# Triangular inversion of the gated delta rule: four doublings on four 32x32 blocks instead of five on two 64x64 blocks

## The chip, the cores and the metric

The kernel runs on one core of a Trainium2 chip. The metric is the device time of one execution in microseconds. TensorE (PE in the profile) multiplies, VectorE (DVE), ScalarE (ACT) and GpSimd (POOL) do the elementwise work, and SyncE (SP) issues the transfers.

## The reference

One decoder layer over 512 positions of width 1024. The normalised input goes through one projection of about 11,300 columns into three branches (differential attention, gated delta rule, cross-attention into 256 memory positions); three output projections are merged by gates, then comes one more projection, and a squared-ReLU MLP of width 4096. The change lies in the gated delta rule of branch B:

```
C = DN_CHUNK                                   # 64 positions in the reference
decay = jnp.exp(jnp.where(causal, G[..., :, None] - G[..., None, :], -jnp.inf))
lower = jnp.where(strict, jnp.einsum('bhnid,bhnjd->bhnij', k_beta, k) * decay, 0.0)
rhs = jnp.concatenate([v_beta, k_beta * jnp.exp(G)[..., None]], axis=-1)
sol = lax.linalg.triangular_solve(lower + jnp.eye(C, dtype=f32), rhs, left_side=True,
                                  lower=True, unit_diagonal=True)
```

The solution is unique in exact arithmetic whatever the length of a chunk; the kernel works with chunks of 128 positions.

## The kernel before, in words

**The weight stream.** All projections are sequences of tiles: 128 output channels by 512 positions (256 for the memory), 8 blocks of 128 input channels each. Every fp32 product is made of three fp32r products (high times high, high times low, low times high), lines L1688 to L1690, into `acc`. The work is cut into pieces of a quarter of a tile (half a tile for the memory), and between two pieces TensorE takes one step of the attention (`attn`, into `ps_a`) or of the delta rule (`delta`, into `ps_d`).

**The delta rule** runs four times, once per pair of heads p. A pair has 2 heads x 4 chunks = 8 matrices of 128x128, and most steps treat all 8 with one small matmul each. `delta_steps()` lists the steps. dv, dk, dq, dqT, dqd, dkT, dkb and dO are transposes; dE, dL, dA, dU and dW are products of 8 full 128x128 matrices; sa and sb are the recurrence over chunks. dL gives the strictly lower matrix (transposed, in `LT`), and between dA and dU its unit triangular system is inverted.

**The inversion** doubles the size of the inverted diagonal blocks: with T the inverse for blocks of one size, the next is T (I - L_level T), L_level being L under a mask that leaves the squares off the diagonal inside blocks of twice the size. So each level has a step Za (L_level times T, subtracted from the unit matrices as it leaves PSUM, giving Y) and a step Wb (Y times T, and the same transposed). T1 is Za of the first level. Levels 1 to 5 work on the two 64x64 blocks of the diagonal of each of the 8 matrices; Zl and Wl then compute the one 64x64 block off the diagonal. The masked matrices of each level (`XT[0]`, `XT[1]`, in buffers SCR and KBT) are made by one 128x1024 operation per level, the first on VectorE (L1491), five on GpSimd (`level_operand`, L883).

**The array.** A matmul whose operands begin at partition 0 or 64 and have 64 rows and 64 output partitions takes one 64x64 tile of the array, so that two on the diagonal can run together. In T1 and Za the two write to different banks (`block_out`), in Wb too (L1817 bank 0, L1820 bank 1).

**The order.** `plan_order` computes ahead of time, from `ORDER` (the sequence of weight tiles) and the tables `PE_US`, `ACT_US`, `DVE_US`, `POOL_US` (planned times), in which order each engine's queue holds its work. In the program that order is fixed, and semaphores carry the dependencies: a step on TensorE waits for the evacuation of the step before it, except as `vector_before` and `pool_before` say. A step that is not ready holds up the weight stream behind it.

## Time and profile before

| | |
|---|---|
| median of 3 runs | 1416.65 us (1414.28 to 1417.52) |
| profiled execution, its own time | 1417.36 us |
| its span, first to last instruction | 1415.5 us |
| TensorE busy | 1380.3 us, 98% |
| VectorE, ScalarE, GpSimd busy | 805.6, 475.2, 245.2 us |
| chain that ended last, share of PE | 93% |

The projections of the mixing part and, between their pieces, all attention and delta steps lie between the start-up and 841 us; the branch outputs, the merge and the MLP follow. A matmul's record begins when it starts to stream and its duration includes the way through the array, so the records of a row overlap; distances between starts tell what a matmul costs the queue. An fp32 matmul leaves two records.

### The profile page before, as it was taken

The page shows a single profiled execution, that of the slowest core. Times are in us where ns is not written, and L with a number is a line of the kernel's source. Part 1 is how long each engine was busy: PE and PEld are TensorE (multiplying, and loading weights), DVE is VectorE, ACT ScalarE, POOL GpSimd, SP SyncE. Part 2 cuts the span into 40 slices and gives each one's busy share as a digit, 9 for nine tenths or more (in the row PEclk, how much of TensorE's full clock was granted, in tenths as well). Part 3 has the DMA queues.
Part 4 walks back from the last instruction along what each step waited for, and adds up shares of the span by engine and source line. Part 5 has one row for each costly group of instructions (what it writes and reads, how often), then busy time and mean ns, then how long its engine had stood idle before and what let it go on. Part 6 is the DMA issues. An engine that isn't in the chain of part 4 may idle for free.

```text
span 1415.5 us, 20801 instructions
## 1 busy us (share of the span) xinstructions
PE 1380.3 (98%) x8692; PEld 1145.9 (81%) x8692; DVE 805.6 (57%) x1264; ACT 475.2 (34%) x742; POOL 245.2 (17%) x156
## 2 busy tenths in 40 slices
PE   5999999999999999999999999999989999999998
PEld 5689887788888888788887878888878888888886
DVE  6796325588935787767865444454356532355342
ACT  5344333334334434444334321122443221232231
POOL 1113100004200122001330142223222200022010
PEclk9999999999999999999999999999989999999998
DMA  5154212222212321123222356644313223322221
GB/s 208 60 178 143 91 60 75 95 85 82 70 60 75 112 68 61 53 68 104 83 68 69 119 180 207 193 157 143 118 45 105 91 88 97 99 102 89 90 89 60
DMA packets 46420, 142.91 MB, mean 101 GB/s; under 512 B 4944, under 2 KB 7416, under 8 KB 46328
## 3 DMA queue, kind: packets, MB, share of 16 engines
q1 hardware_dynamic: 46328, 141.59, 30.1%
q8 instruction: 69, 1.13, 0.3%
q14 instruction: 23, 0.19, 0.0%
HBM read 126.88 MB, written 16.27 MB: 101 GB/s over the span
## 4 chain that ended last, share of the span: by engine, by line
PE 93%; DVE 5%; ACT 1%; issue 1%; DMA 0%; DVEq 0%; POOL 0%; SPq 0%; ACTq 0%
PE acc L1688 25%; PE acc L1690 24%; PE acc L1689 24%; PE ps_d L1830 2%; PE ps_d L1812 2%; PE ps_d L1817 2%; PE ps_a L1763 2%; PE ps_a L1774 1%; PE ps_d L1802 1%; PE ps_d L1820 1%; DVE conv_y L1383 1%; PE ps_a L1742 1%; PE ps_a L1753 1%; DVE w_lo L1285 1%; PE ps_d L1797 1%; PE ps_a L1769 1%
## 5 line engine op out<-in xcount | busy, mean ns | idle before, releaser
L1688 PE MATMUL acc<-n_hi,w_hi 128*128 128x512 f32 (+1 forms) x984 | 396.7, 403 | 7.4 <-DVE n_lo L1310 4.3
L1690 PE MATMUL acc<-n_hi,w_lo 128*128 128x512 f32 (+1 forms) x984 | 383.3, 390 | 0.0
L1689 PE MATMUL acc<-n_lo,w_hi 128*128 128x512 f32 (+1 forms) x984 | 382.9, 389 | 0.0
L1285 DVE TENSOR_TENSOR w_lo<-w_raw,w_hi 128x1024 fp32r<-128x1024 f32 x200 | 284.4, 1429 | 141.9 <-ACT w_hi L996 141.3
L996 ACT CAST w_hi<-w_raw 128x1024 fp32r<-128x1024 f32 x200 | 209.4, 1048 | 456.3 <-PE acc L1690 456.3
L1688 PEld LDWEIGHTS acc<-n_hi,w_hi 128*128 128x128 f32 x984 | 188.0, 191 | 49.0 <-issue 8.8
L1690 PEld LDWEIGHTS acc<-n_hi,w_lo 128*128 128x128 f32 x984 | 187.7, 191 | 40.5
L1689 PEld LDWEIGHTS acc<-n_lo,w_hi 128*128 128x128 f32 x984 | 188.4, 191 | 34.7 <-issue 0.2
L1690 PE MATMUL acc<-h_hi,w_lo 128*128 128x512 f32 x256 | 101.0, 395 | 0.0
L1688 PE MATMUL acc<-h_hi,w_hi 128*128 128x512 f32 x256 | 101.0, 395 | 0.0
L1689 PE MATMUL acc<-h_lo,w_hi 128*128 128x512 f32 x256 | 101.0, 395 | 0.0
L984 POOL TENSOR_TENSOR h_lo<-sq,h_hi 128x512 fp32r<-128x512 f32 x32 | 41.4, 1293 | 234.0 <-DVE h_hi L1619 234.0
L1688 PE MATMUL acc<-y_hi,w_hi 128*128 128x512 f32 x192 | 76.1, 396 | 0.7 <-ACT gate_st L1075 0.7
L1690 PE MATMUL acc<-y_hi,w_lo 128*128 128x512 f32 x192 | 76.0, 396 | 0.0
L1689 PE MATMUL acc<-y_lo,w_hi 128*128 128x512 f32 x192 | 76.0, 396 | 0.0
L926 POOL TENSOR_SCALAR gate_st<-gate_st 128x512 f32<-128x512 f32 x24 | 25.1, 1045 | 286.8 <-ACT gate_st L1075 286.8
L1230 ACT ACTIVATE sq<-relu 128x512 f32<-128x512 f32 x32 | 20.2, 632 | 125.2 <-DVE relu L1617 125.2
L1383 DVE SCALAR_TENSOR_TENSOR conv_y<-conv_x,par,conv_y 128x512 f32<-128x512 f32 x72 | 59.4, 825 | 2.6
L1690 PEld LDWEIGHTS acc<-h_hi,w_lo 128*128 128x128 f32 x256 | 48.2, 188 | 11.3
L1688 PEld LDWEIGHTS acc<-h_hi,w_hi 128*128 128x128 f32 x256 | 48.2, 188 | 11.2
L1689 PEld LDWEIGHTS acc<-h_lo,w_hi 128*128 128x128 f32 x256 | 48.2, 188 | 11.2
L1617 DVE TENSOR_SCALAR relu<-acc 128x512 f32<-128x512 f32 x31 | 21.4, 691 | 39.8 <-PE acc L1690 39.8
(322 smaller groups left out, 2051.8 us busy)
## 6 DMA issues: line engine op xcount, KB each, us to landing
w_raw<-weights SPq DMA_DIRECT2D x200, 512.0 KB, 3.3
gate_scratch<-gate_st SPq DMA_DIRECT2D x24, 256.0 KB, 2.2
g_in<-gate_scratch SPq DMA_DIRECT2D x24, 256.0 KB, 3.7
y_raw<-y_scratch SPq DMA_DIRECT2D x16, 256.0 KB, 3.5
x_tok<-x SPq DMA_DIRECT2D x4, 512.0 KB, 5.1
y_scratch<-y_st SPq DMA_DIRECT2D x4, 512.0 KB, 3.0
y_scratch<-d_ET SPq DMA_DIRECT2D x4, 512.0 KB, 3.2
y_scratch<-y_st SPq DMA_DIRECT2D x8, 256.0 KB, 3.5
```

What stands on the lines that cost most here:

```text
L926: nc.gpsimd.tensor_scalar(gate_st[:], gate_st[:], 0.5, 0.5, ALU.mult, ALU.add).then_inc(gs_ready, 1)
L984: nc.gpsimd.tensor_tensor(h_lo[:, f % 16], sq[:, f % 2], h_hi[:, f % 16].bitcast(F32), ALU.subtract).then_inc(hl_ok, 1)
L996: nc.scalar.copy(w_hi[:, t % SPL], w_raw[:, t % RAW]).then_inc(hi_ready, 1)
L1285: V_.tensor_tensor(w_lo[:, t % SPL], w_raw[:, t % RAW], w_hi[:, t % SPL].bitcast(F32), ALU.subtract).then_inc(lo_ready, 1)
L1383: ins = V_.scalar_tensor_tensor(out=y, in0=conv_x[:, n % 2, j:j + S], scalar=par[:, col + j:col + j + 1], in1=y, op0=ALU.mult, op1=ALU.add)
L1688: mm(bank, wh, hi_of(k), start=start and k == 0, stop=False)
L1689: mm(bank, wh, lo_of(k), start=False, stop=False)
L1690: last = mm(bank, wl, hi_of(k), start=False, stop=stop and k == KT - 1)
L1763: last = mm(ps[:, col:col + (q + 1) * P], qkv_T[rows_m, h % 2, 0, q * P:(q + 1) * P], qkv_T[rows_m, h % 2, 1, 0:(q + 1) * P], start=True, ...
L1812: last = mm(block_out(m, s), XT[c % 2][HP[s], m, HP[s]], right, start=True, stop=True)
L1817: last = mm(ps_d[HP[s], 0, c0:c0 + P // 2], Y[HP[s], m], TP[HP[s], m], start=True, stop=True)
L1830: last = mm(dst[m], a[:, m], b[:, m], start=True, stop=True)
```

## The change

- The levels 1 to 4 (T1, four Za, four Wb) work on the four 32x32 diagonal blocks of each matrix, one matmul per block: 32 per step and product instead of 16. Their operands are packed: 32 columns per matrix, 256 in all, in each buffer. All four blocks of a product go to one bank (`small_out`).
- Level 5 is now two steps like the last level: Z5 and W5 compute the 32x32 blocks off the diagonal inside each 64x64 block. ScalarE puts the result together in TF (six small operations).
- Zl takes its right-hand side from two buffers (TR for the first 32 columns with 64 rows of contraction, TN for the other 32 columns with 32 rows), so it has 16 matmuls instead of 8. Wl is as before.
- ScalarE copies the diagonal blocks of LT into LD (four copies), and one GpSimd operation multiplies LD with the masks of all four levels; five operations fall away. GpSimd clears the whole TF instead of half.
- T1 stands right behind dL in the list of steps. `scalar_before` is new and lets steps wait for an earlier ScalarE part.
- A one-time set-up on VectorE moves mask blocks together and adds up four unit blocks instead of two.
- `ORDER` and the planned times are new, so all queues of the mixing part are ordered anew.

```diff
-         "dkb": "AP", "dL": "DP", "dA": "DP", "T1": "DP", "Za": "DP", "Wb": "AD", "Zl": "A", "Wl": "D",
+         "dkb": "AP", "dL": "ADP", "dA": "DP", "T1": "D", "Za": "D", "Wb": "AD", "Z5": "A", "W5": "AD", "Zl": "A", "Wl": "D",
-PE_US = {"dE": 1.79, "dL": 1.79, "dA": 1.79, "dU": 1.79, "dW": 1.79, "T1": 0.95, "Za": 0.95, "Wb": 1.85, "Zl": 0.95, "Wl": 0.95, "sa": 0.45,
+PE_US = {"dE": 1.79, "dL": 1.79, "dA": 1.79, "dU": 1.79, "dW": 1.79, "T1": 0.55, "Za": 0.55, "Wb": 1.05, "Z5": 0.55, "W5": 0.8, "Zl": 0.95, "Wl": 0.95, "sa": 0.45,
-ACT_US = {"Wb": 0.75, "Zl": 0.62, "sb": 0.45, "cs": 2.9, "as0": 2.3, "as1": 2.9, "at": 1.5, "ap": 0.65,
+ACT_US = {"dL": 1.6, "Wb": 0.45, "Z5": 0.45, "W5": 2.1, "Zl": 0.62, "sb": 0.45, "cs": 2.9, "as0": 2.3, "as1": 2.9, "at": 1.5, "ap": 0.65,
-DVE_US = {"dv": 1.3, "dk": 7.8, "dq": 6.5, "dqT": 1.3, "dL": 2.6, "dA": 2.7, "T1": 0.8, "Za": 0.8, "Wb": 0.8, "Wl": 0.8, "sa": 0.5, "sb": 0.8,
+DVE_US = {"dv": 1.3, "dk": 7.8, "dq": 6.5, "dqT": 1.3, "dL": 2.9, "dA": 1.9, "T1": 0.5, "Za": 0.5, "Wb": 0.6, "W5": 0.5, "Wl": 0.8, "sa": 0.5, "sb": 0.8,
-POOL_US = {"dk": 2.0, "dkT": 2.0, "dkb": 2.0, "dL": 2.5, "dA": 3.8, "T1": 2.5, "Za": 2.5}
+POOL_US = {"dk": 2.0, "dkT": 2.0, "dkb": 2.0, "dL": 2.5, "dA": 4.5}
...
-ORDER = [("conv", 0), ("z", 0), ("gate", 1), ("mem", 0), ("cq", 0), ("cq", 1), ("cq", 2), ("cq", 3),
+ORDER = [("conv", 0), ("gate", 1), ("z", 0), ("mem", 0), ("cq", 0), ("cq", 1), ("cq", 2), ("conv", 1),
...
-        out += [(k, p, 0) for k in ("dv", "dk", "dq", "dE", "dkT", "dkb", "dL", "dqT", "dA", "dqd", "T1")]
-        for lv in range(1, NM - 1):
+        out += [(k, p, 0) for k in ("dv", "dk", "dq", "dE", "dkT", "dkb", "dL", "T1", "dqT", "dA", "dqd")]
+        for lv in range(1, 5):
             out += [("Za", p, lv), ("Wb", p, lv)]
-        out += [("Zl", p, NM - 1), ("Wl", p, NM - 1), ("dU", p, 0), ("dW", p, 0)]
+        out += [("Z5", p, 5), ("W5", p, 5), ("Zl", p, 6), ("Wl", p, 6), ("dU", p, 0), ("dW", p, 0)]
...
-            "dA": ("dL", p, 0), "dqd": ("dqT", p, 0), "T1": ("dqT", p, 0)}.get(kind)
+            "T1": ("dL", p, 0), "dqT": ("dL", p, 0), "dA": ("dL", p, 0), "dqd": ("dqT", p, 0)}.get(kind)
+
+
+def scalar_before(step):
+
+    kind, p, c = step
+    if kind == "Za":
+        return ("dkb", p, 0) if c == 1 else ("dqd", p, 0) if c == 2 else ("Wb", p, c - 2)
+    return {"T1": ("dkb", p, 0), "Z5": ("Wb", p, 3), "Zl": ("Z5", p, 5)}.get(kind)
 
 
 def pool_before(step):
 
     kind, p, c = step
-    if kind == "Za" and c > 2:
-        return ("Za", p, c - 2)
     return {("dE", 0): ("dk", p, 0), ("dW", 0): ("dkb", p, 0), ("sb", 0): ("dA", p, 0),
-            ("Za", 1): ("dL", p, 0), ("Za", 2): ("T1", p, 0), ("dU", 0): ("dA", p, 0)}.get((kind, c))
+            ("Za", 1): ("dL", p, 0), ("dU", 0): ("dA", p, 0)}.get((kind, c))
...
-        XT = (SCR, KBT)
-        TP, TN = (flat(TT[:])[:, n * 512:(n + 1) * 512].rearrange("p (a b) -> p a b", b=P // 2) for n in range(2))
-        Y = flat(KTT[:])[:, 0:512].rearrange("p (a b) -> p a b", b=P // 2)
         HP = (slice(0, P // 2), slice(P // 2, P))
-        two_eyes = cst[:, C_MASK0 + NM - 1, HP[0]]
+        QB = P // 4
+        BLK = [slice(q * QB, (q + 1) * QB) for q in range(4)]
+
+        def part_of(buf, n, width=QB):
+            return flat(buf[:])[:, n * 256:n * 256 + 8 * width].rearrange("p (a b) -> p a b", b=width)
+
+        X0, LD = part_of(KBT, 0), part_of(KBT, 1)
+        XS = flat(SCR[:]).rearrange("p (l a b) -> p l a b", l=4, b=QB)
+        TP, TN, TR = (part_of(TT, n) for n in range(3))
+        Y, Y5, Y6 = part_of(KTT, 0), part_of(KTT, 1), part_of(KTT, 2, P // 2)
+        eyes = cst[:, C_MASK0 + NM - 1, 0:QB]
...
+        def small_out(bank, rows=slice(0, P)):
+
+            return ps_d[rows, bank, 0:256].rearrange("p (a b) -> p a b", b=QB)
+
+        def mid_out(bank, rows):
+
+            return ps_d[rows, bank].rearrange("p (a b) -> p a b", b=P // 2)
...
-                    pool.wait_ge(d_dve, dD[i + 1])
-                    last = level_operand(1)
+                    pool.wait_ge(d_act, dA[i + 1])
+                    last = nc.gpsimd.tensor_tensor(XS, view(LD, [[0, 4], [QB, 8], [1, QB]]),
+                                                   view(cst[:, C_MASK0 + 1, 0:QB], [[P, 4], [0, 8], [1, QB]]), ALU.mult)
                 elif kind == "dA":
                     pool.wait_ge(at_ready, p + 1)
                     nc.gpsimd.tensor_tensor(AT[:], AT[:], over(cst[:, C_UPTO, :], 8), ALU.mult)
-                    last = nc.gpsimd.memset(TF[:, :, HP[0]], 0.0)
-                elif kind == "T1":
-                    pool.wait_ge(d_dve, dD[d_idx[("dA", p, 0)] + 1])
-                    last = level_operand(2)
-                elif kind == "Za":
-                    last = level_operand(lv + 2)
...
+                elif kind == "dL":
+                    act.wait_ge(d_dve, dD[i + 1])
+                    for q in range(4):
+                        last = nc.scalar.copy(LD[BLK[q]], LT[BLK[q], :, BLK[q]])
                 elif kind == "Wb":
-                    for s in range(2):
-                        last = nc.scalar.copy(TF[HP[s], :, HP[s]], whole_bank(0, HP[s]))
+                    last = nc.scalar.copy(TP, small_out(0))
+                elif kind == "Z5":
+                    last = nc.scalar.copy(Y5, small_out(2))
+                elif kind == "W5":
+                    act.wait_ge(d_pool, dP[d_idx[("dA", p, 0)] + 1])
+                    for q in range(4):
+                        nc.scalar.copy(TF[BLK[q], :, BLK[q]], TP[BLK[q]])
+                    for q in (0, 2):
+                        last = nc.scalar.mul(TF[BLK[q], :, BLK[q + 1]], small_out(0, BLK[q]), -1.0)
                 elif kind == "Zl":
-                    last = nc.scalar.copy(by_bank(Y[HP[1]]), blocks_of(HP[1]))
+                    last = nc.scalar.copy(Y6[HP[1]], mid_out(2, HP[1]))
...
-                link(V_.tensor_tensor(two_eyes, ident[:, HP[0]], ident[:, HP[1]], ALU.add))
+                for q in range(1, 4):
+                    V_.tensor_copy(cst[BLK[q], C_MASK0:C_MASK0 + 5, 0:QB], cst[BLK[q], C_MASK0:C_MASK0 + 5, BLK[q]])
+                link(V_.tensor_tensor(eyes, ident[:, BLK[0]], ident[:, BLK[1]], ALU.add))
+                for q in range(2, 4):
+                    link(V_.tensor_tensor(eyes, eyes, ident[:, BLK[q]], ALU.add))
...
-                    last = V_.tensor_tensor(XT[0][:], LT[:], over(cst[:, C_MASK0, :], 8), ALU.mult)
+                    for q in range(4):
+                        last = V_.tensor_tensor(X0[BLK[q]], LT[BLK[q], :, BLK[q]], over(cst[BLK[q], C_MASK0, 0:QB], 8), ALU.mult)
                 elif kind == "dA":
                     V_.tensor_tensor(AT[:], ps, ET[:], ALU.mult).then_inc(at_ready, 1)
-                    for s in range(2):
-                        last = V_.tensor_tensor(TP[HP[s]], over(two_eyes[HP[s]], 8), XT[0][HP[s], :, HP[s]], ALU.subtract)
+                    last = V_.tensor_tensor(TP, over(eyes, 8), X0, ALU.subtract)
                 elif kind in ("T1", "Za"):
-                    eyes = view(two_eyes, [[0, 2], [0, 4], [1, P // 2]])
-                    last = V_.tensor_tensor(by_bank(TN if kind == "T1" else Y), eyes, blocks_of(), ALU.subtract)
+                    last = V_.tensor_tensor(TN if kind == "T1" else Y, over(eyes, 8), small_out(2), ALU.subtract)
                 elif kind == "Wb":
-                    rows = slice(0, P) if c < NM - 2 else HP[0]
-                    last = V_.tensor_copy(TN[rows], whole_bank(1, rows))
+                    last = V_.tensor_copy(TN, small_out(1))
+                    if c == 4:
+                        last = V_.tensor_copy(TR[BLK[0]], small_out(1, BLK[0]))
+                elif kind == "W5":
+                    last = V_.tensor_scalar(TR[BLK[1]], small_out(1, BLK[1]), -1.0, None, ALU.mult)
                 elif kind == "Wl":
-                    last = V_.tensor_scalar(by_bank(TF[HP[0], :, HP[1]]), blocks_of(HP[0]), -1.0, None, ALU.mult)
+                    last = V_.tensor_scalar(TF[HP[0], :, HP[1]], mid_out(0, HP[0]), -1.0, None, ALU.mult)
...
-                    for k in range(8):
-                        for s, m in ((0, k), (1, (k + 4) % 8)):
-                            right = ident[HP[s], HP[s]] if kind == "T1" else TN[HP[s], m]
-                            last = mm(block_out(m, s), XT[c % 2][HP[s], m, HP[s]], right, start=True, stop=True)
+                    for m in range(8):
+                        for b in BLK:
+                            left, right = (X0[b, m], eyes[b]) if kind == "T1" else (XS[b, c - 1, m], TN[b, m])
+                            last = mm(small_out(2, b)[:, m], left, right, start=True, stop=True)
                 elif kind == "Wb":
-                    for s in range(2):
-                        for m in range(8):
-                            c0 = m * (P // 2)
-                            last = mm(ps_d[HP[s], 0, c0:c0 + P // 2], Y[HP[s], m], TP[HP[s], m], start=True, stop=True)
-                            if c < NM - 2 or s == 1:
-                                o = HP[1 - s]
-                                last = mm(ps_d[o, 1, c0:c0 + P // 2], TP[o, m], Y[o, m], start=True, stop=True)
+                    for m in range(8):
+                        for b in BLK:
+                            mm(small_out(0, b)[:, m], Y[b, m], TP[b, m], start=True, stop=True)
+                        for b in BLK:
+                            last = mm(small_out(1, b)[:, m], TP[b, m], Y[b, m], start=True, stop=True)
+                elif kind == "Z5":
+                    for m in range(8):
+                        for q in (0, 2):
+                            last = mm(small_out(2, BLK[q + 1])[:, m], LT[BLK[q], m, BLK[q + 1]], TN[BLK[q], m],
+                                      start=True, stop=True)
+                elif kind == "W5":
+                    for m in range(8):
+                        for q in (0, 2):
+                            mm(small_out(0, BLK[q])[:, m], Y5[BLK[q + 1], m], TP[BLK[q + 1], m], start=True, stop=True)
+                        last = mm(small_out(1, BLK[1])[:, m], TP[BLK[1], m], Y5[BLK[1], m], start=True, stop=True)
                 elif kind == "Zl":
                     for m in range(8):
-                        last = mm(block_out(m, 1), LT[HP[0], m, HP[1]], TN[HP[0], m], start=True, stop=True)
+                        mm(mid_out(2, HP[1])[:, m, 0:QB], LT[HP[0], m, HP[1]], TR[HP[0], m], start=True, stop=True)
+                        last = mm(mid_out(2, HP[1])[:, m, QB:], LT[BLK[1], m, HP[1]], TN[BLK[1], m], start=True, stop=True)
                 elif kind == "Wl":
                     for m in range(8):
-                        last = mm(block_out(m, 0), Y[HP[1], m], TF[HP[1], m, HP[1]], start=True, stop=True)
+                        last = mm(mid_out(0, HP[0])[:, m], Y6[HP[1], m], TF[HP[1], m, HP[1]], start=True, stop=True)
```

Two places on TensorE and one on VectorE, as the programs hold them; names as in the code, `d_` for the buffers of the delta rule, and the last column is what a row writes (xN: N such in a row).

TensorE, the step Wb of level 1 of the first pair, before:

```order
L1688 MATMUL acc<-m_hi,w_hi 128x256
L1689 MATMUL acc<-m_lo,w_hi 128x256
L1690 MATMUL acc<-m_hi,w_lo 128x256
L1817 MATMUL ps_d<-d_TT,d_KTT 64x64
L1820 MATMUL ps_d<-d_KTT,d_TT 64x64
```

and after:

```order
L1698 MATMUL acc<-m_hi,w_hi 128x256
L1699 MATMUL acc<-m_lo,w_hi 128x256
L1700 MATMUL acc<-m_hi,w_lo 128x256
L1828 MATMUL ps_d<-d_TT,d_KTT 32x32 x4
L1830 MATMUL ps_d<-d_KTT,d_TT 32x32 x4
```

The last two rows come 16 times in the one and 8 times in the other program, so the step has 32 matmuls before and 64 after; alternating blocks of 64x64 in two banks have become groups of four blocks in one bank.

TensorE, the step Zl, of the first pair, before:

```order
L1689 MATMUL acc<-n_lo,w_hi 128x512
L1690 MATMUL acc<-n_hi,w_lo 128x512
L1823 MATMUL ps_d<-d_TT,d_LT 64x64 x8
L1688 MATMUL acc<-n_hi,w_hi 128x512
L1689 MATMUL acc<-n_lo,w_hi 128x512
```

and after:

```order
L1699 MATMUL acc<-m_lo,w_hi 128x256
L1700 MATMUL acc<-m_hi,w_lo 128x256
L1843 MATMUL ps_d<-d_TT,d_LT 64x32
L1844 MATMUL ps_d<-d_TT,d_LT 64x32
L1843 MATMUL ps_d<-d_TT,d_LT 64x32
```

L1843 contracts over 64 rows and L1844 over 32; they alternate eight times, where one kind stood in a row.

VectorE, the one-time set-up, before:

```order
L1352 TENSOR_TENSOR smd<-smd 128x1
L1353 TENSOR_SCALAR smd<-smd 128x1
L1355 TENSOR_TENSOR cst<-cst 128x64
L1357 TENSOR_SCALAR beta<-ba 128x32
L1358 TENSOR_SCALAR hbeta<-ba 128x32
```

and after:

```order
L1356 TENSOR_TENSOR smd<-smd 128x1
L1357 TENSOR_SCALAR smd<-smd 128x1
L1360 COPY cst<-cst 32x5x32 x3
L1361 TENSOR_TENSOR cst<-cst 128x32
L1363 TENSOR_TENSOR cst<-cst 128x32 x2
L1365 TENSOR_SCALAR beta<-ba 128x32
```

One addition has become three copies and three additions ahead of the decay's computation.

## Rows read from the trace of the kernel before

**Rows 1.** The page: busy time and share, then TensorE's granted clock in 40 slices.

```profile
PE 1380.3 (98%) x8692; PEld 1145.9 (81%) x8692; DVE 805.6 (57%) x1264; ACT 475.2 (34%) x742; POOL 245.2 (17%) x156
PEclk9999999999999999999999999999989999999998
```

**Rows 2.** Table by window, the mixing part from 60 to 840 us.

```profile
core 0: us, PE busy (x) PEld busy (x) DVE busy (x) ACT busy (x) POOL busy (x), PEclk, DMA share, GB/s
60.00:840.00 780.00, 777.40 (x5882) 648.77 (x5881) 518.00 (x876) 300.58 (x522) 126.11 (x70) 1.00 0.27 90
```

**Rows 3.** Waits of TensorE: waiting line, releaser, us in total, times, longest.

```profile
PE ps_a L1649 <- DVE x_tok L1297: 10.0, 1, 10.0
...
PE ps_d L1797 <- DVE conv_o L1397: 1.2, 1, 1.2
...
PE ps_d L1797 <- DVE d_V L1485: 0.7, 1, 0.7
```

**Rows 4.** Timeline of TensorE, a Wb step: start, us, line, shapes, count.

```profile
136.19 0.28 PE L1690 MATMUL acc<-m_hi,w_lo 128*128 128x256 f32 x1
...
136.51 0.22 PE L1817 MATMUL ps_d<-d_TT,d_KTT 64*64 64x64 f32 x1
136.52 0.22 PE L1820 MATMUL ps_d<-d_KTT,d_TT 64*64 64x64 f32 x1
136.57 0.22 PE L1817 MATMUL ps_d<-d_TT,d_KTT 64*64 64x64 f32 x1
...
138.42 0.38 PE L1688 MATMUL acc<-m_hi,w_hi 128*128 128x256 f32 x1
138.64 0.28 PE L1689 MATMUL acc<-m_lo,w_hi 128*128 128x256 f32 x1
```

**Rows 5.** Timeline of TensorE, the T1 step.

```profile
127.92 0.28 PE L1690 MATMUL acc<-m_hi,w_lo 128*128 128x256 f32 x1
128.13 1.15 PE L1812 MATMUL ps_d<-cst,d_SCR 64*64 64x64 f32 x32
...
129.43 0.28 PE L1689 MATMUL acc<-m_lo,w_hi 128*128 128x256 f32 x1
```

**Rows 6.** Timeline of TensorE, the dL step of full 128x128 matrices.

```profile
109.82 0.28 PE L1690 MATMUL acc<-m_hi,w_lo 128*128 128x256 f32 x1
109.94 1.95 PE L1830 MATMUL ps_d<-d_KBT,d_KTT 128*128 128x128 f32 x16
...
111.84 0.28 PE L1689 MATMUL acc<-m_lo,w_hi 128*128 128x256 f32 x1
```

**Rows 7.** Timeline of TensorE, a score step: 64 rows, 128 columns of the array.

```profile
474.59 0.39 PE L1689 MATMUL acc<-n_lo,w_hi 128*128 128x512 f32 x1
474.82 0.40 PE L1690 MATMUL acc<-n_hi,w_lo 128*128 128x512 f32 x1
475.15 1.56 PE L1763 MATMUL ps_a<-qkv_T 64*128 64x384 f32 x10
...
476.98 0.39 PE L1689 MATMUL acc<-n_lo,w_hi 128*128 128x512 f32 x1
```

**Rows 8.** Timeline of TensorE, the Zl step, one 64x64 tile.

```profile
176.31 0.40 PE L1690 MATMUL acc<-n_hi,w_lo 128*128 128x512 f32 x1
176.64 1.14 PE L1823 MATMUL ps_d<-d_TT,d_LT 64*64 64x64 f32 x16
...
178.05 0.39 PE L1689 MATMUL acc<-n_lo,w_hi 128*128 128x512 f32 x1
```

**Rows 9.** Groups by line and form: busy us, mean ns, idle before, releaser.

```profile
L1506 DVE TENSOR_TENSOR vnew<-d_Q,ps_d 128x256 f32<-128x256 f32 x12 | 5.0, 419 | 14.5 <-PE ps_d L1833 14.5
L1137 ACT COPY d_LT<-ps_d 128x256 f32<-128x256 f32 x16 | 6.0, 373 | 25.7 <-PE ps_d L1843 25.7
L883 POOL TENSOR_TENSOR d_KBT<-d_LT,cst 128x1024 f32<-128x1024 f32 x12 | 28.8, 2400 | 75.7 <-PE ps_d L1812 53.5 <-DVE d_SCR L1491 22.2
```

**Rows 10.** Timeline of VectorE, the one-time set-up.

```profile
61.09 0.22 DVE L1355 TENSOR_TENSOR cst<-cst 128x64 f32<-128x64 f32 x1
```

**Rows 11.** Timeline of GpSimd, its last piece of the first branch's reload.

```profile
837.09 2.21 POOL L920 TENSOR_TENSOR y_lo<-y_st,y_hi 128x512 fp32r<-128x512 f32 x1 [1.53 <-DVE y_hi L1532]
```

More of the change, by code:

```diff
@@ L83 @@
 HOP, MARGIN = 0.2, 0.5
-ORDER = [("conv", 0), ("z", 0), ("gate", 1), ("mem", 0), ("cq", 0), ("cq", 1), ("cq", 2), ("cq", 3),
-         ("conv", 1), ("head", 0), ("gate", 3), ("conv", 2), ("head", 1), ("gate", 2), ("head", 2), ("z", 1),
-         ("gate", 2), ("head", 3), ("head", 4), ("conv", 3), ("head", 5), ("z", 2), ("gate", 2), ("head", 6),
-         ("gate", 3), ("head", 7), ("gate", 2), ("z", 3), ("gate", 9)]
+ORDER = [("conv", 0), ("gate", 1), ("z", 0), ("mem", 0), ("cq", 0), ("cq", 1), ("cq", 2), ("conv", 1),
+         ("gate", 1), ("cq", 3), ("gate", 1), ("head", 0), ("gate", 1), ("conv", 2), ("head", 1), ("gate", 1),
+         ("head", 2), ("z", 1), ("gate", 2), ("head", 3), ("gate", 1), ("head", 4), ("conv", 3), ("head", 5),
+         ("z", 2), ("gate", 3), ("head", 6), ("head", 7), ("gate", 2), ("z", 3), ("gate", 11)]
 def attn_steps():
@@ L257, in plan_order @@
         kind, p, c = s
-        deps = [("ACT", "delta", j) for j in range(i) if "A" in PARTS[delta[j][0]]][-1:]
+        after = scalar_before(s)
+        j = i if after is None else d_idx[after] + 1
+        deps = [("ACT", "delta", j) for j in range(j) if "A" in PARTS[delta[j][0]]][-1:]
         after = vector_before(s)
@@ L279, in plan_order @@
             add("DVE", "delta", ("delta", i), DVE_US["sb_last" if end else kind], deps)
-        if "P" in PARTS[kind] and not (kind == "Za" and c + 2 >= NM - 1):
+        if "P" in PARTS[kind]:
             deps = [mm]
-            if kind == "T1":
-                deps.append(("DVE", "delta", d_idx[("dA", p, 0)]))
             if kind == "dL":
-                deps.append(("DVE", "delta", i))
+                deps.append(("ACT", "delta", i))
             if kind == "dA":
@@ L379, in counts @@
     for s in steps:
-        last_levels = part == "P" and s[0] == "Za" and s[2] + 2 >= NM - 1
-        out.append(out[-1] + (part in PARTS[s[0]] and not last_levels))
+        out.append(out[-1] + (part in PARTS[s[0]]))
     return out
@@ L879, in _ @@
                 nc.gpsimd.tensor_tensor(lo, full[:, j % 4], hi.bitcast(F32), ALU.subtract).then_inc(su_lo, 1)
-            def level_operand(lv):
-                return nc.gpsimd.tensor_tensor(XT[lv % 2][:], LT[:], over(cst[:, C_MASK0 + lv, :], 8), ALU.mult)
             def delta(i):
@@ L887, in delta @@
                 if "P" not in PARTS[kind]:
-                    return
-                if kind == "Za" and lv + 2 >= NM - 1:
                     return
@@ L908, in delta @@
                     nc.gpsimd.tensor_tensor(AT[:], AT[:], over(cst[:, C_UPTO, :], 8), ALU.mult)
-                    last = nc.gpsimd.memset(TF[:, :, HP[0]], 0.0)
-                elif kind == "T1":
-                    pool.wait_ge(d_dve, dD[d_idx[("dA", p, 0)] + 1])
-                    last = level_operand(2)
-                elif kind == "Za":
-                    last = level_operand(lv + 2)
+                    last = nc.gpsimd.memset(TF[:], 0.0)
                 last.then_inc(d_pool, 1)
@@ L1782, in delta @@
                 kind, p, c = DELTA[i]
-                if dA[i]:
-                    pe.wait_ge(d_act, dA[i])
+                before = scalar_before(DELTA[i])
+                n_act = dA[i] if before is None else dA[d_idx[before] + 1]
+                if n_act:
+                    pe.wait_ge(d_act, n_act)
                 before = vector_before(DELTA[i])
```

13 lines of the change are left out of this document (1 added, 12 removed).

## The prediction

> **What bounds the kernel now.** I read the busy shares first: TensorE is busy 1380.3 of 1415.5 us, and the row of its granted clock is 9 nearly throughout, the full 2.4 GHz level, with two slices of 8 [rows 1]. Then the stretch in which all of the change lies, from 60 to 840 us (tables by window): TensorE busy 777.40 of 780.00 us at clock 1.00, VectorE 518.00, ScalarE 300.58, GpSimd 126.11 [rows 2]. Then what TensorE waits for: the long waits are in the start-up, and inside the stretch only 1.2 and 0.7 us stand out, both on VectorE near 78 and 94 us [rows 3]. So TensorE's queue is the path. A microsecond less in it is a microsecond less in the kernel, a microsecond less on the three other engines is worth nothing, and they matter only if they come late.
>
> **What a small step costs today.** I take a step's price as what it inserts between two products of the weight stream: the start of the second product behind it, less the start of the last one ahead, less two normal distances (0.12 us for 256 columns, 0.23 for 512). The last product's successor on either side shows the distances [rows 6, 7].
> - 128x128, 8 matrices, 16 records (each fp32 matmul leaves two): 111.84 - 109.82 - 0.24 = 1.78 us, 0.111 a record, nothing left over [rows 6].
> - T1 or Za, 16 matmuls on two 64x64 tiles: 129.43 - 127.92 - 0.24 = 1.27 us for 32 records, which is 16 turns of two [rows 5].
> - Wb, 32 matmuls: 138.64 - 136.19 - 0.24 = 2.21 us for 32 turns of two [rows 4].
> - Zl, 8 matmuls on one tile: 178.05 - 176.31 - 0.46 = 1.28 us for 16 turns of one [rows 8]. The same as T1: the second tile rides along free.
> The last two sizes give slope and offset: (2.21 - 1.27)/16 = 0.0588 us a turn, and 1.27 - 16 x 0.0588 = 0.33 us a step, which the 128x128 step does not have. I read the 0.33 as two changes of the array's division, 0.165 each. A change of the rows alone costs it too: the score step with 64 rows and all 128 columns inserts 476.98 - 474.82 - 0.46 = 1.70 us [rows 7]; of its ten records four have 128 data columns (0.111 each), two 256 (0.12) and four 384 (0.16 at 2.4 GHz), 1.32 us, and 0.38 are left over.
> Per pair of heads: T1 and five Za 7.62, five Wb 11.05 (I price the last, shorter one alike), Zl and Wl 2.55: 21.2 us.
>
> **What it costs after.** From 128 to 64 a turn fell from 0.111 to 0.0588, by 0.052 for 64 columns of weights and 64 of data. Half of that less gives 0.0326 us for 32x32: an estimate from rows 4 to 6. The number of turns is the program's: 8 matrices x 2 records, whatever the number of blocks, if four blocks share a turn as two do now.
> - T1 and four Za: 5 x (0.33 + 16 x 0.0326) = 4.26 us.
> - Four Wb, 32 turns: 4 x (0.33 + 32 x 0.0326) = 5.49.
> - Z5, 16 turns of two: 0.85. W5: two of its three matmuls for a matrix read the same 32 rows, so 32 turns: 1.37.
> - Zl: it now alternates, per matrix, a matmul with 64 contraction rows and one with 32, so 16 matmuls on one group of columns. Weights are 64 columns and data 32, midway between the two turns: 0.0457 x 32 = 1.46, plus 0.33. And the division changes 15 times inside the step. No row has such a change inside a step. Lower bound: nothing, if only the size 128 against smaller counts; upper: 15 x 0.165 = 2.48 us. I take the upper, since a change of the rows alone is enough in [rows 7]. Zl: 4.27.
> - Wl as now: 1.27.
> Sum 17.5 us a pair, 3.7 less, 14.8 us over four pairs.
>
> **The other engines.** Evacuations shrink from 512 to 256 columns: a 256-column VectorE operation with a PSUM source takes 419 ns, ScalarE's 373 [rows 9]. Five masks of 2400 ns per pair on GpSimd become one; all that was hidden and gains nothing. New: four small copies on ScalarE behind the LT product, about 4 x 0.37 = 1.5 us, then the one GpSimd mask, 2.4. Za 1 waits for it; T1, dqT, dA and dqd with their weight products lie between, at least 0.85 + 0.87 + 1.79 + 0.87 us of steps plus four pieces of the stream at about 1.4 us: some 10 us against 5.1 (1.2 + 1.5 + 2.4). Hidden. W5's ScalarE part is six operations, 2.2 us; Zl doesn't wait for it, only Wl, behind Zl and a piece of the stream: hidden. What is queued behind it on ScalarE is the next weight split, which has whole tiles of slack. If these covers were gone, each would cost its excess, 1 to 2 us a pair.
> The set-up on VectorE (the one-time block at 61 us) has one addition of 0.22 us now [rows 10] and gets three copies and three additions: by bounds 0.22 (64 columns) and 0.42 (256) the copies are about 0.3, the additions 0.2, so +1.3 us. VectorE has no slack there: TensorE's waits of 0.7 and 1.2 us follow [rows 3]. Between nothing and 1.3 I take 1.3.
> The new ORDER moves weight tiles among each other; products and loads stay the same in number. After the last attention step six gate tiles are left instead of seven, 5.5 us less cover for the reload of the first branch. GpSimd now finishes its last y_lo at 839.3 us [rows 11], and that piece is needed 4.8 us after the branch's start near 841.5: margin 7 us, then 1.5. Priced at nothing; gone, it costs up to 2.
> Sum: 14.8 - 1.3 = 13.5 us. The profiled execution took 1417.36 us, 0.71 over the median of the runs shown, so 1403.9 in its terms and **1403 us** in terms of the median.
>
> **A rule against it.** The two records of a pair start at 136.51 and 136.52, about 0.01 us apart, and the turn is 0.0588, so two starts average 0.029 us [rows 4]. Now the two blocks of a turn write to different PSUM banks; after it, four write to one bank, in different partitions. The Trainium skill, TensorEngine Tiling (Array Packing), Restrictions and Gotchas, says that different row tiles cannot access the same bank at once. TensorE: Matmul & The Clock Gate, Part 1, gives about 25 ns as the least distance of starts. By an estimate with that page's 25 ns per start the four-block steps and Z5 and W5 would take the kernel to about 1461 us instead of 1403. The trace shows a shorter distance than this between two tiles, though not on average, and nothing about one bank; what a limit on starts does here is priced from rows as the second rival.
>
> **Rivals.**
> 1. *Changes inside Zl are free.* For: rows 4 to 8 show only changes from and to 128. Against: rows alone suffice [rows 7]. Saves 2.48 x 4 = 9.9 us more: 1393 us.
> 2. *Four blocks don't share a turn: slower.* The mechanism: a start each 0.029 us, the average of today, is the engine's or the bank's limit. Then a turn of four is 0.118: T1 and Za 5 x 2.22 = 11.1, Wb 4 x 4.11 = 16.4, Z5 1.26, W5 1.72, Zl 4.27, Wl 1.27, together 36.0 us a pair, 14.8 more: +59 us, plus the set-up, 1477 us. It decides from a turn of about 0.033 + 3.7/208 = 0.050 us, 208 being the four-block turns of a pair. For: twice as many instructions per step as now, at a rate that no row shows sustained. Against: the 0.01 us inside a pair.
> 3. *The other engines come late or the turn is 0.04 to 0.05.* 13 dependent steps in a shorter chain, now planned against smaller numbers; 0.2 us at each of 52 steps is 10 us: 1413 us. Against: 2.6 us without TensorE work in 780 today [rows 2].
>
> **Numbers.** Chances: forecast 0.40 (its own range 1398 to 1408), rival 1 0.22, rival 2 0.18, rival 3 0.20. The runs shown span 1414.28 to 1417.52, so 0.2% is about what tells from no change: faster means below 1413.8. Faster: 0.40 + 0.22 + 0.12 of rival 3 = 0.74; same 0.05; slower 0.18 + 0.03 = 0.21. The range 1389 to 1418 leaves out rival 2 and the edges of 1 and 3.
>
> **What would show it.** Za's records in turns of four, 0.03 us apart, and the step inserting 0.85 instead of 1.27 us; Zl about 4 us long (rival 1: under 2); no group of small matmuls with a turn above 0.05; TensorE's waits between 60 and 840 us not above 5 us in sum; the end of the gates near 828 us. The forecast is wrong if four blocks queue behind each other, or if the reordered tiles leave TensorE waiting.

## The result, and the profile after

The changed kernel takes 1429.31 us (median of 5 runs, 1423.33 to 1432.13) against 1416.12 of the kernel before (5 runs beside it, 1414.04 to 1417.52): ratio 1.0083, 95% interval 1.0069 to 1.0097. It is slower, where 1403 had been forecast. Its profiled execution took 1424.05 us, 5.3 less than the median of its runs, so the traces below show the loss at its small end.

The page of the kernel after, busy times, TensorE's granted clock, and the queue that carries instructions (packets, MB, share of the DMA engines):

```profile
PE 1370.4 (96%) x10420; PEld 1133.2 (80%) x10420; DVE 772.8 (54%) x1277; ACT 482.7 (34%) x778; POOL 202.2 (14%) x140
PEclk9999999999999999999998999999989999999999
q8 instruction: 83, 1.36, 0.4%
```

The same queue on the page of the kernel before:

```profile
q8 instruction: 69, 1.13, 0.3%
```

TensorE is busy for 9.9 us less than in [rows 1] and the kernel is longer. The table by window says where:

```profile
60.00:840.00 780.00, 761.67 (x7566) 632.47 (x7565) 476.79 (x880) 304.95 (x554) 76.59 (x48) 0.98 0.28 87
530.00:545.00 15.00, 12.70 (x358) 9.64 (x357) 5.43 (x11) 3.55 (x6) 0.00 (x0) 0.89 0.27 86
740.00:785.00 45.00, 43.15 (x592) 34.17 (x591) 16.25 (x35) 14.41 (x28) 1.16 (x1) 0.85 0.21 66
```

Against [rows 2], TensorE now stands idle for 18.3 us of 780 instead of 2.6, and the clock, 1.00 before, is 0.98, with 0.89 and 0.85 in two places. Rows of what it waits for (line, releaser, us, times, longest):

```profile
PE ps_d L1830 <- issue: 4.2, 3, 2.3
PE ps_d L1828 <- issue: 4.2, 4, 1.9
...
PE ps_d L1824 <- issue: 3.0, 4, 1.1
PE acc L1698 <- issue: 2.8, 2, 2.5
...
PE acc L1699 <- issue: 0.9, 1, 0.9
```

These 15.1 us are new beside [rows 3], and their releaser is "issue": no semaphore, no engine. L1824 is T1 and Za, L1828 and L1830 are Wb, L1698 and L1699 are the weight stream. The timeline of TensorE through one Wb (start, us, line, shapes, count):

```profile
144.76 0.28 PE L1700 MATMUL acc<-m_hi,w_lo 128*128 128x256 f32 x1
144.97 0.26 PE L1828 MATMUL ps_d<-d_TT,d_KTT 32*32 32x32 f32 x8
...
145.81 0.21 PE L1828 MATMUL ps_d<-d_TT,d_KTT 32*32 32x32 f32 x2
147.94 0.22 PE L1828 MATMUL ps_d<-d_TT,d_KTT 32*32 32x32 f32 x2 [1.92 <-issue]
...
148.31 0.38 PE L1698 MATMUL acc<-m_hi,w_hi 128*128 128x256 f32 x1
```

and through the next Za:

```profile
149.71 0.28 PE L1700 MATMUL acc<-m_hi,w_lo 128*128 128x256 f32 x1
149.91 0.75 PE L1824 MATMUL ps_d<-d_TT,d_SCR 32*32 32x32 f32 x64
150.60 0.39 PE L1698 MATMUL acc<-m_hi,w_hi 128*128 128x256 f32 x1
150.82 0.28 PE L1699 MATMUL acc<-m_lo,w_hi 128*128 128x256 f32 x1
```

The Za inserts 150.82 - 149.71 - 0.24 = 0.87 us, as forecast (0.85): four blocks do share a turn. The Wb ran at the same pace and then stood still for 2.1 us in the middle of a matrix. The trace has eleven such distances of over 0.7 us between two starts from 100 to 850 us, 16.5 us in all; before has one, 1.05 us.

The trace's records of the instruction queue point to the cause. Each packet has 16,384 bytes; 83 of them for 2 x 10420 TensorE instructions (a load of weights and a matmul each) makes 251 to a packet, the few waits and register instructions not counted. I take it as 256 of 64 bytes; the array probe below, which pauses every 256 instructions, bears this out. Beside the standstills of the first pair:

```
packet starts   takes   TensorE's next start after a standstill
132.98          1.03    135.45
137.23          0.96    139.40
140.56          1.12    143.11
145.18          1.28    147.94
```

Each of the eleven standstills ends 1.1 to 1.6 us after a packet does, and no two packets start less than 3.3 us apart; in the kernel before none start less than 5.3 us apart. A Wb is 256 instructions, issued in 1.1 us.

Zl, beside [rows 8]:

```profile
160.47 0.28 PE L1700 MATMUL acc<-m_hi,w_lo 128*128 128x256 f32 x1
160.67 0.30 PE L1843 MATMUL ps_d<-d_TT,d_LT 64*64 64x32 f32 x2
160.90 0.30 PE L1844 MATMUL ps_d<-d_TT,d_LT 32*64 32x32 f32 x2
...
164.37 0.58 PE L1698 MATMUL acc<-m_hi,w_hi 128*128 128x256 f32 x1
164.75 0.41 PE L1699 MATMUL acc<-m_lo,w_hi 128*128 128x256 f32 x1
164.96 0.41 PE L1700 MATMUL acc<-m_hi,w_lo 128*128 128x256 f32 x1
```

It inserts 4.0 us (4.27 forecast), and behind it the stream's products stand 0.21 us apart instead of 0.12: from 164.2 to 167.6 us the granted clock is 0.5, the 1.2 GHz level. There are five such stretches between 27 and 1030 us where before has none: behind or in Zl of three pairs (3.4, 3.4 and 10.2 us) and behind the two standstills of 2.5 and 1.8 us at 533.6 and 748.6 us (3.4 us each), 23.8 us together. The first product of the branch comes at 850.05 us instead of 841.57, 8.5 later. From there the two kernels take the same time to within 0.4 us up to the last 35 us, in which this execution of the changed kernel is 1.4 us quicker.

### The profile page after: what moved, and what is told of

Same layout as the page of the kernel before. It is cut to its first block, busy times and chain, and to the rows that moved or that the text cites. A ratio compares the mean times of both kernels' runs of the same rounds, so it can differ in the third digit from the quotient of the medians.

```text
span 1422.3 us, 24294 instructions
## 1 busy us (share of the span) xinstructions
PE 1370.4 (96%) x10420; PEld 1133.2 (80%) x10420; DVE 772.8 (54%) x1277; ACT 482.7 (34%) x778; POOL 202.2 (14%) x140
## 4 chain that ended last, share of the span: by engine, by line
PE 91%; DVE 5%; issue 2%; ACT 1%; DMA 0%; DVEq 0%; POOL 0%; SPq 0%; ACTq 0%
PE acc L1698 25%; PE acc L1700 24%; PE acc L1699 24%; PE ps_d L1851 2%; PE ps_a L1773 2%; PE ps_a L1784 1%; PE ps_d L1814 1%; DVE conv_y L1391 1%; PE ps_d L1824 1%; PE ps_a L1763 1%; PE ps_a L1752 1%; DVE w_lo L1289 1%; PE ps_d L1828 1%; PE ps_d L1830 1%; PE ps_d L1809 1%
## 5 line engine op out<-in xcount | busy, mean ns | idle before, releaser
L1698 PE MATMUL acc<-n_hi,w_hi 128*128 128x512 f32 (+1 forms) x984 | 398.2, 405 | 10.8 <-DVE n_lo L1314 4.3
L1699 PE MATMUL acc<-n_lo,w_hi 128*128 128x512 f32 (+1 forms) x984 | 385.0, 391 | 0.0
L1698 PEld LDWEIGHTS acc<-n_hi,w_hi 128*128 128x128 f32 x984 | 188.9, 192 | 48.8 <-issue 8.8
L1699 PEld LDWEIGHTS acc<-n_lo,w_hi 128*128 128x128 f32 x984 | 189.3, 192 | 38.8 <-issue 3.3
L1698 PE MATMUL acc<-h_hi,w_hi 128*128 128x512 f32 x256 | 101.0, 395 | 0.0
L1699 PE MATMUL acc<-h_lo,w_hi 128*128 128x512 f32 x256 | 101.0, 395 | 0.0
L1698 PE MATMUL acc<-y_hi,w_hi 128*128 128x512 f32 x192 | 76.0, 396 | 0.0
L1699 PE MATMUL acc<-y_lo,w_hi 128*128 128x512 f32 x192 | 76.0, 396 | 0.0
L1699 PEld LDWEIGHTS acc<-h_lo,w_hi 128*128 128x128 f32 x256 | 48.2, 188 | 11.3
L1698 PEld LDWEIGHTS acc<-h_hi,w_hi 128*128 128x128 f32 x256 | 48.2, 188 | 11.2
L1698 PEld LDWEIGHTS acc<-y_hi,w_hi 128*128 128x128 f32 x192 | 36.2, 188 | 8.9 <-POOL y_lo L915 0.2
```

What stands on the lines that cost most here:

```text
L1698: mm(bank, wh, hi_of(k), start=start and k == 0, stop=False)
L1699: mm(bank, wh, lo_of(k), start=False, stop=False)
```

## The experiments

Theory F: TensorE passes the array steps faster than its instructions arrive. Theory Z: the alternation in Zl costs more than its own time, through the clock. Rival O: the new order of the stream. Two more rivals stand in the expectations: B, that four blocks which write to one bank hold each other up, and C, that other transfers hold back the packets of instructions.

**Zl in products of one size (zl_one_size).** TR takes 64 columns, a block of it is zeroed, and the second matmul of each matrix goes:

```diff
-mm(mid_out(2, HP[1])[:, m, 0:QB], LT[HP[0], m, HP[1]], TR[HP[0], m], start=True, stop=True)
-last = mm(mid_out(2, HP[1])[:, m, QB:], LT[BLK[1], m, HP[1]], TN[BLK[1], m], start=True, stop=True)
+last = mm(mid_out(2, HP[1])[:, m], LT[HP[0], m, HP[1]], TR[HP[0], m], start=True, stop=True)
...
```

> Zl's right-hand side is put into one buffer of 64 columns per matrix (32 rows of it cleared by GpSimd), so Zl is 8 matmuls of one size again; everything else as in the changed kernel. In the changed kernel's trace Zl inserts 3.95 and 4.08 us where it inserted 1.28 before. Theory Z (the alternation of 64 and 32 contraction rows is paid at every change): Zl inserts 1.3 us, four times 2.7 us less, 10.9 us, and the half-clock window that begins at the first Zl (164 us) goes, 1.7 us: 1416 to 1418 us from 1429. Theory F (TensorE runs out of instructions) alone: the stalls inside Za and Wb stay where they are, 12 to 17 us in sum. Rival O (the cost lies in the new order of the queues): no change, 1429 us.

Measured 1406.55 us (1401.75 to 1412.91), ratio 0.9936 [0.9917, 0.9955]. The timeline of Zl:

```profile
163.29 0.28 PE L1703 MATMUL acc<-m_hi,w_lo 128*128 128x256 f32 x1
163.50 1.14 PE L1846 MATMUL ps_d<-d_TT,d_LT 64*64 64x64 f32 x16
164.57 0.39 PE L1701 MATMUL acc<-m_hi,w_hi 128*128 128x256 f32 x1
164.79 0.28 PE L1702 MATMUL acc<-m_lo,w_hi 128*128 128x256 f32 x1
```

164.79 - 163.29 - 0.24 = 1.26 us, 2.8 less than in this pair above, some 11 over four. Mixing, from the stream's first product to the branch's first, shrank by 21.5 us (829.4 to 807.9), twice that, and the median lies 10 us under the expectation. Ten distances of over 0.7 us remain, 13.4 us in all against 16.5, which is another 3. The rest, some 7.5 us, goes with the clock: one stretch of 3.4 us at half clock is left of 23.8 us. But two of the five stretches had stood behind a standstill and not behind Zl. So Z holds, and more than Zl's own time was saved; how much of the 21.5 us each part gave is an estimate.

**Wb as two steps (wb_in_two).** The order of the stream stays; each Wb is issued as 128 and 128 instructions with a piece of the stream between.

```diff
-out += [("Za", p, lv), ("Wb", p, lv)]
+out += [("Za", p, lv), ("Wa", p, lv), ("Wb", p, lv)]
...
+if e == "PE" and fam == "delta" and delta[q[0][2]][0] == "Wb":
+    ready = max(ready, done[("PE", "delta", q[0][2] - 1)] + 0.6)
```

> The changed kernel with Wb as two steps, its two products of 32 matmuls each, between which the planner is made to put a piece of the weight stream; no matmul more or less. Theory F (a burst of 256 instructions outruns the loads of instructions): costs 16 more entries to the small division at 0.33 us, 5.3 us, and takes the stalls inside Wb away, of 14 to 17 us at least 10, and with them the two half-clock windows at 536 and 751 us, 3.4 us: 1429 + 5 - 10 - 4 = 1420 us, idle of TensorE between 100 and 840 us without a semaphore under 5 us. Rival B (the stalls come from four blocks that write to one bank): the products are the same, so the stalls stay and the entries come on top: 1434 us. Rival O: about 1434 us too.

Measured 1413.37 us (1408.97 to 1418.69), ratio 0.9982 [0.9971, 0.9993], below the expectation. Distances over 0.7 us fell from eleven (16.5 us) to three (3.8 us), and the two half-clock stretches behind the standstills at 533.6 and 748.6 us are gone; 17 us at half clock remain elsewhere. Same instructions, two more changes of the array's division for each Wb, and faster by 15.9 us: F holds, and rival B, which expected 1434, falls.

**The old kernel in the new order (before_new_order).** Only the list ORDER is exchanged; its first rows:

```diff
-ORDER = [("conv", 0), ("z", 0), ("gate", 1), ("mem", 0), ("cq", 0), ("cq", 1), ("cq", 2), ("cq", 3),
+ORDER = [("conv", 0), ("gate", 1), ("z", 0), ("mem", 0), ("cq", 0), ("cq", 1), ("cq", 2), ("conv", 1),
```

> The kernel before with the changed kernel's list ORDER of weight tiles, and its own steps and planned times. Rival O (the new order of tiles makes the other engines late): 1424 to 1430 us. Theories F and Z: the order costs nothing, 1416 us, within 2 us.

Measured 1421.65 us (1420.02 to 1428.19), ratio 1.005 [1.0031, 1.0068]. TensorE's waits:

```profile
PE acc L1688 <- POOL y_lo L920: 4.5, 3, 2.2
```

They stand at 849.7, 851.7 and 854.9 us: the reload of the first branch comes too late, the margin that I had priced at nothing. This profiled execution took 1428.19 us, 6.5 above the median, and has a stretch of 6.8 us at half clock behind these waits, so how much of them the other executions have isn't known. The changed kernel's profile has no wait of this kind. With the shorter steps, mixing and reload meet otherwise.

**The changed kernel in the old order (after_old_order)**: the same exchange, the other way.

```diff
-ORDER = [("conv", 0), ("gate", 1), ("z", 0), ("mem", 0), ("cq", 0), ("cq", 1), ("cq", 2), ("conv", 1),
+ORDER = [("conv", 0), ("z", 0), ("gate", 1), ("mem", 0), ("cq", 0), ("cq", 1), ("cq", 2), ("cq", 3),
```

> The changed kernel with the stream's order list of the kernel before (the list alone; the planner places the steps in it). Theory O (the new list is what costs: before_new_order was 5 us slower than before): 5 us or more below the changed kernel, 1418 to 1424 us. Theory F (the list is innocent, since the changed kernel's profile has none of the waits at L1688 for y_lo, 4.5 us, that before_new_order shows): within 3 us of the changed kernel's 1429 us, as far as the stalls fall alike.

Measured 1424.03 us (1420.05 to 1425.76), ratio 1.0059 [1.0038, 1.008]. Rows of its waits:

```profile
PE ps_d L1828 <- issue: 4.9, 2, 3.2
PE acc L1698 <- POOL y_lo L915: 4.0, 3, 2.3
...
PE ps_d L1824 <- issue: 1.9, 2, 1.1
```

With the old list the changed kernel has 4.0 us of waits for y_lo and fewer "issue" waits. The four medians read as a square: the new steps cost 7.7 us in the old order (1424.03 against 1416.31) and 7.7 in the new (1429.31 against 1421.65); the new list costs 5.6 us with the old steps and 5.3 with the new. So the order is not the main cause, but it is some 5 of the 13 us by which the median rose, more than the 3 that I had allowed. The 5.3 us is not clear of noise: the runs of the changed kernel in its two orders overlap (1420.05 to 1425.76 and 1423.33 to 1432.13). Which wait carries it was not separated.

**The array alone (array_probe).** No layer is computed: TensorE repeats bursts between wide products, without semaphores or other engines, and x is copied to the output. The first burst:

```python
for m in range(64):
    for q in range(4):
        mm(ps[Q4[q], 0, 0:32], a[Q4[q], 0:32], a[Q4[q], 32:64], start=True, stop=True)
```

> A kernel of TensorE bursts alone, without the layer: its output is a copy of x. Between stretches of fp32 128x512 matmuls: 256 matmuls of 32x32 on the four diagonal blocks into one bank; the same into four banks; 256 of 64x64 on two blocks into two banks; 128 of these into one bank; a burst of 32 of 32x32; 16 that alternate 64 and 32 contraction rows; 16 of 64 rows. Theory F: every long burst is bound by the loads of instructions, 1024 instructions in at least four times 2.5 us once the stock is used up, with gaps every 256 instructions of 1 us and more for 32x32 (whose own pace is 1.06 us per 256), none for 64x64 (3.7 us per 256), and the one-bank burst like the four-bank burst. Rival B: the one-bank burst slower per turn than the four-bank one, steadily. Theory Z: 16 alternating matmuls take about 3.7 us, 16 of one size under 1.5. The clock goes to its lower level where the bursts have gaps.

By window: 256 products of 32x32 in four blocks, into one bank; the same into four banks; 256 products of 64x64 in two blocks.

```profile
31.00:43.00 12.00, 6.50 (x514) 5.80 (x512) 0.00 (x0) 0.78 0.02 5
66.00:78.00 12.00, 5.82 (x500) 5.21 (x500) 0.00 (x0) 0.74 0.02 4
101.00:116.00 15.00, 15.00 (x513) 14.98 (x512) 0.00 (x0) 1.00 0.02 4
```

512 records of 32x32 take 11.5 us from first to last start and TensorE works for half of it; the same number of 64x64 takes 14.9 us without a pause. Within the burst a turn of four blocks takes 0.034 us, in one bank as in four, which rules out rival B. But after the first 163 records in the one burst, 243 in the other, and then every 128 (256 instructions), comes a pause of 1.8 to 2.6 us, so such a block takes 3.4 to 3.7 us. A turn of two 64x64 blocks takes 0.0585, so 128 records take 3.7 us, and the supply just keeps up. The clock falls to 0.5 in or behind both bursts of 32x32, for 10.2 us each, as expected, and stays at 1.00 through the bursts of 64x64. An alternating Zl takes 3.64 us there, sixteen products of a single size 1.98: 0.11 us for each of 15 changes, at full clock.

**The step's cycle alone (cycle_probe).** Also without a layer:

```python
for n in (6, 12):
    for c in range(8):
        small(8)     # 32 products of 32x32, as Za
        piece(n)     # n products, 128x128 by 160 columns
        small(16)    # 64 products, as Wb
        piece(n)
    fill(24)
```

> No layer is computed and x is copied to the output: TensorE alone repeats the burst cycle of the array steps (32 products of 32x32, a piece of 12 records of stream products, 64 products of 32x32, a piece), eight times with the pieces as they stand in the changed kernel's first pair and eight times with twice the piece; then Zl's sixteen products with alternating tile sizes and Zl's products of one size, four times each with a piece of 24 records between. No semaphore stands in any of it and no other engine works. Theory F (supply of instructions alone): a short cycle has 432 instructions, of which 256 take 3.4 us to arrive, so it takes 5.7 us instead of the 5.1 us it takes without a stall, in gaps of 1 to 2.5 us, and the long cycle (480 instructions, 6.4 us to arrive, 8.3 us of work) has none over 0.3 us once it runs. Rival C (the stalls in the layer come from the other DMA traffic that holds back the instruction packets): short cycles too run without a gap at 5.1 us. For the clock: half-clock stretches behind the short cycles and in the alternating Zl, none in the long cycles and none in the Zl of one size; alternating Zl inserts 3.6 us and Zl of one size 1.0 to 1.3 us.

The timeline of the short cycle:

```profile
40.59 1.27 PE L46 MATMUL ps<-a 32*32 32x32 f32 x127
42.68 0.18 PE L46 MATMUL ps<-a 32*32 32x32 f32 x1 [0.82 <-issue]
42.79 1.90 PE L41 MATMUL big<-a 128*128 128x160 f32 x12
44.62 0.75 PE L46 MATMUL ps<-a 32*32 32x32 f32 x64
```

and by window the short cycles, the long ones, the alternating Zl with 24 records of the stream behind each, the Zl of one size with the same:

```profile
32.00:82.00 50.00, 46.22 (x1728) 41.71 (x1728) 0.00 (x0) 1.00 0.02 5
102.00:173.00 71.00, 71.00 (x1921) 67.01 (x1920) 0.00 (x0) 1.00 0.01 3
194.00:234.00 40.00, 40.00 (x221) 36.40 (x221) 0.00 (x0) 0.66 0.00 0
255.00:273.00 18.00, 18.00 (x159) 16.92 (x159) 0.00 (x0) 1.00 0.00 1
```

A short cycle takes 6.2 us on average, 5.55 where nothing stops it; the long one 8.8 with TensorE busy throughout. The DMA engines carry nothing else there (5 GB/s), so the supply of instructions alone makes the pauses: rival C falls as the sole cause. In the layer's first pair they add up to 6.7 us over three and a half cycles, 1.9 a cycle against 0.7 here. The packets themselves take no longer there (0.9 to 1.3 us in both), nor does the restart behind them (1.2 to 1.5 us, here 1.3 to 1.6); it is the next packet that starts later after a restart, 1.2 to 2.8 us in that pair and 1.0 to 1.6 here. Why was not isolated. For the clock the expectation was half wrong: short cycles leave it at 1.00. The alternating Zl draws it to half each time, for 6.8 us (mean 0.66). Such a Zl with its piece takes 10.2 us and one of a single size 4.5: 5.6 us apart. The layer's two versions are 21.5/4 = 5.4 apart, but that is near by luck in part: there one Zl of four left the clock alone, and fewer pauses are in the sum.

**More stream between the steps (after_spaced, zl_spaced).** The instructions are the same (zl_spaced adds the edit of zl_one_size); the planner puts two pieces instead of one ahead of most Za and Wb.

```diff
+if e == "PE" and fam == "delta" and delta[q[0][2]][0] in ("Za", "Wb"):
+    ready = max(ready, done[("PE", "delta", q[0][2] - 1)] + 1.6)
```

> The changed kernel, with only the order planner told that a Za or Wb may start no sooner than 1.6 us of its own count after the step before it on TensorE, which puts two stream pieces instead of one between most of these steps. The same instructions, in another order, and no step is split. Theory F (the array steps run ahead of the supply of instructions: a 16,384-byte block of 256 arrives every 3.4 us at best in the probe, and one cycle of Za, piece, Wb, piece consumes 432 instructions in 5.1 us): the gaps of 0.7 to 2.6 us without a semaphore, 16.4 us of them in the changed kernel's profile, shrink below 4 us, the two stretches at half clock behind the stalls at 533 and 748 us go, those in Zl stay, and the median comes to 1411 to 1417 us. Theory N (the stalls are a fixed cost of each Za and Wb, however they are spread): 1427 to 1432 us.

Measured 1421.3 us (1414.68 to 1428.34), ratio 1.004 [1.002, 1.0059]: the right direction, and half of what F had promised, so a miss. In its waits:

```profile
PE ps_d L1830 <- issue: 2.8, 1, 2.8
...
PE ps_d L1826 <- DVE d_KBT L1502: 1.8, 1, 1.8
...
PE acc L1700 <- issue: 1.7, 1, 1.7
```

Pauses without a semaphore remain, 6.6 us where under 4 was expected, one of nearly 3 us, with 3.4 us at half clock behind it; and the new order brings a wait on VectorE. A block of 256 instructions is not one step; that spacing the steps does not space the blocks is my reading, and no run tests it by itself.

> zl_one_size together with the spacing of after_spaced. Theory F and Z together (the losses are the instruction supply and Zl's alternation, and they add): 12 to 15 us below zl_one_size, 1390 to 1396 us, with stretches at half clock gone between 30 and 1000 us. If the two causes overlap (both only through the clock): 1400 to 1405 us. If longer chains of steps bring new waits at the end of mixing (the planner's own end moves 2.4 us): 2 to 3 us above the first range.

Measured 1399.13 us (1398.85 to 1400.29), ratio 0.9887 [0.9872, 0.9902]: 7.4 us below zl_one_size, 3 above the expected range. The half-clock stretches between 30 and 1000 us are gone, and 3.6 us of "issue" waits are left.

**Both remedies (zl_and_wb)**: the two diffs of zl_one_size and wb_in_two together.

> zl_one_size together with wb_in_two: Wb is issued as two steps of 128 instructions with a stream piece between, at a price of two more changes of array division for each of 16 steps (16 x 0.33 = 5.3 us). Theory F with Z: the stalls go and 5.3 us are paid, so 4 to 6 us above zl_spaced, 1394 to 1400 us. If the split is not the cause of wb_in_two's gain but its order is: no more than 3 us below zl_one_size, 1403 to 1407 us.

Measured 1397.27 us (1394.11 to 1398.71), ratio 0.9869 [0.9854, 0.9885]: the fastest of all, 1.3% below the kernel before. It is 9.3 us under zl_one_size, where 3 at most had been expected if not the split but its order helped. Rows of this kernel's page, and its window:

```profile
PE 1359.3 (98%) x10356; PEld 1122.7 (81%) x10356; DVE 770.7 (55%) x1281; ACT 482.5 (35%) x778; POOL 204.4 (15%) x144
PEclk9999999999999999999999999999989999999998
60.00:840.00 780.00, 775.61 (x7633) 640.67 (x7632) 490.95 (x903) 313.09 (x564) 89.19 (x62) 1.00 0.30 96
```

No distance of over 0.7 us is left between 100 and 850 us, and the clock is 1.00. By the prices measured, a pair costs 5 x 0.88 (T1, Za) + 8 x 0.88 (Wb halves) + 2 x 0.82 (Z5, W5) + 2 x 1.27 (Zl, Wl) = 15.6 us against 21.2 before: 22.3 over four pairs. Mixing measures 799.4 against 821.0 us: 21.6.

## Why the prediction was wrong, by its steps

- **TensorE's queue is the path.** Right: none of the other engines became the bound in the changed kernel. The set-up on VectorE did grow by 1.2 us (1.3 forecast), but it also began 1.1 us earlier in the new order, and TensorE's two waits behind it are 1.0 and 0.7 us, no longer than in [rows 3]: the term of +1.3 was nothing.
- **The price of a step is what it inserts; four blocks share a turn.** Right. T1 and Za 0.88 (0.85 forecast), an undisturbed Wb 1.41 (1.37), a turn of 0.034 us (0.0326) in one bank. Rival 2, a start each 0.029 us, fell, one bank cost nothing, and with rival 2 fell the reading of the Trainium skill's floor of about 25 ns between starts (TensorE: Matmul & The Clock Gate, Part 1) across blocks: here a start comes every 0.0085 us on average (0.034/4). W5 was mis-sized: 0.82 us, not 1.37.
- **Zl 4.27.** 3.84 in the second pair, where the clock stays up (376.82 to 381.00 us, less distances of 0.11 and 0.23), and 4.04 in the first; changes inside a step do cost, and rival 1 fell. What failed is that nothing was put behind it: "at 2.4 GHz" was taken for granted for whatever follows. In the cycle probe 5.6 us separate the two forms of Zl, of which the alternation itself is some 2.6 (3.64 in the array probe less 1.07 for eight products of 64x64).
- **The step that failed** is the sum's first assumption, that a step costs its turns and two changes. In [rows 2] TensorE passes 5882 records in 780 us, 256 instructions in 17 us on average, and no row that stands ahead of the prediction shows its instructions as a resource, though the page of before has their queue, with 69 packets. Nothing in the sum asked how fast they come. Rival 2 names "twice as many instructions per step" as a doubt, but prices it as a limit on starts in the engine or the bank, and no rival as a limit on their supply. They come 256 in 3.4 us at best, and Za, piece, Wb, piece wants 432 in 5.1. The Trainium skill, Advanced Engine Details and Errata, ISA Cache, states lines of 16 KB for 256 instructions and "Only 2 cache lines!"; the packets of 16,384 bytes agree with the line. The same section gives TensorE 128 KB, which would be eight such lines; no run shows such a stock at work, and in the array probe a burst of 1024 instructions paused after 326. Two lines would have made a rival. The section gives no time, and the 3.4 us is this case's.
- **The order priced at nothing.** This term failed too. By the medians the new list costs about 5 us with either steps. The margin of the reload fails in the old kernel with the new list and in the changed kernel with the old one, and not in the changed kernel as it stands. The other engines cost nothing there that the waits of TensorE show.
- **The account.** Forecast -14.8 in mixing; W5 -2.2; Zl, at 3.84, -1.7; waits for "issue" +15.1; 23.8 us at half clock, which by an estimate from the cycle probe cost about 45% of their length (3.1 of 6.8 us, the 5.6 less 2.57 of alternation), +10.7. Sum +7.1, measured +8.4 (829.4 against 821.0). The order has no term of its own here: whatever it cost in this execution lies within the last two. The median lies another 5 us higher: the runs of the changed kernel spread over 8.8 us and those of before over 3.5, which fits pauses that fall differently from run to run, but only one execution was profiled, so this is not shown.

The chances gave "slower" 0.21, to slow turns and late engines, neither of which happened.
